# Sixteen bytes between the channel chunks of a matmul operand in a hybrid pool, convolution, attention and expert trunk

## The reference, cut to what matters

```
for l in range(DEPTH):
    h = rms_norm(x, g_mix[l])
    u = jnp.einsum('bsd,dc->bsc', h, w_in[l])
    y_pool, y_conv, y_attn, gates = ...
    merged = (gates[:, :, 0] * jnp.einsum('bsc,cd->bsd', y_pool, w_br_pool[l]) + ... )
    x = x + jnp.einsum('bsd,de->bse', merged, w_out[l])
    h = rms_norm(x, g_ffn[l])
    x = x + (swiglu(h, ...) if l % 2 == 0 else moe_ffn(h, ...))
```

## Time and profile before

| | us |
|---|---|
| median of 2 runs | 1742.53 |
| the two runs | 1741.94 and 1743.11 |
| span of the profiled execution, first to last instruction | 1738.7 |
| TensorE busy (matmuls) | 1689.6 (97%) |
| TensorE weight loads busy | 1454.0 (84%) |
| VectorE busy | 1283.2 (74%) |
| ScalarE busy | 1053.3 (61%) |

### The profile page before, as it was taken

How to read it: one execution, slowest core, us unless ns; L and a number is a source line. 1 busy time by engine, 2 the same in 40 slices (tenths; PEclk the granted TensorE clock), 3 DMA queues, 4 the chain that set the end, 5 groups by cost and what they waited for, 6 DMA issues and landing times.

```text
span 1738.7 us, 25143 instructions
## 1 busy us (share of the span) xinstructions
PE 1689.6 (97%) x9630; PEld 1454.0 (84%) x9630; DVE 1283.2 (74%) x1078; ACT 1053.3 (61%) x902; POOL 51.5 (3%) x52
## 2 busy tenths in 40 slices
PE   7999989999899998999999999999999999999998
PEld 7988889999898888788788788788788788788787
DVE  5964754444696475787887887887887887887886
ACT  5544444444554445677677677677677677677675
POOL 0131000000013000000000000000000000000000
PEclk9999999999999998999999999999999999999999
DMA  9533445555353342699899899899899899899893
GB/s 331 172 123 105 142 142 170 193 174 165 122 170 122 116 141 86 253 369 342 316 363 335 323 366 329 333 364 329 319 375 330 327 368 331 324 370 330 322 373 146
DMA packets 231292, 452.46 MB, mean 260 GB/s; under 512 B 6992, under 2 KB 80720, under 8 KB 231120
## 3 DMA queue, kind: packets, MB, share of 16 engines
q1 hardware_dynamic: 231248, 451.82, 73.5%
HBM read 450.74 MB, written 1.05 MB: 260 GB/s over the span
## 4 chain that ended last, share of the span: by engine, by line
PE 89%; DVE 8%; issue 2%; ACT 1%; DVEq 0%; DMA 0%; ACTq 0%
PE bank L269 27%; PE bank L271 27%; PE bank L270 27%; DVE w_low L259 3%; PE bank L1237 2%; PE bank L1253 1%; DVE xacc L929 1%; PE bank L997 1%; DVE h_full L690 1%; PE bank L1087 1%; DVE gate L685 1%; DVE h_full L616 0%; PE bank L1106 0%; ACT w_high L255 0%; DVE rinv L606 0%
## 5 line engine op out<-in xcount | busy, mean ns | idle before, releaser
L259 DVE TENSOR_TENSOR w_low<-raw,w_high 128x2048 fp32r<-128x2048 f32 x427 | 975.5, 2290 | 323.8 <-ACT w_high L255 322.8
L255 ACT ACTIVATE w_high<-raw 128x2048 fp32r<-128x2048 f32 x427 | 818.3, 1917 | 441.6 <-PE bank L271 439.6
L269 PE MATMUL bank<-w_high,hg_high 128*128 128x512 f32 x896 | 358.5, 400 | 7.6 <-DVE w_low L259 7.6
L270 PE MATMUL bank<-w_low,hg_high 128*128 128x512 f32 x896 | 353.9, 395 | 0.0
L271 PE MATMUL bank<-w_high,hg_low 128*128 128x512 f32 x896 | 353.9, 395 | 0.0
L269 PE MATMUL bank<-h_high,w_high 128*128 128x256 f32 x1056 | 307.3, 291 | 9.4 <-DVE h_low L611 4.8
L270 PE MATMUL bank<-h_low,w_high 128*128 128x256 f32 x1056 | 300.9, 285 | 0.0
L271 PE MATMUL bank<-h_high,w_low 128*128 128x256 f32 x1056 | 300.9, 285 | 0.0
L269 PEld LDWEIGHTS bank<-h_high,w_high 128*128 128x128 f32 x1056 | 204.8, 194 | 15.0 <-issue 9.6
L269 PEld LDWEIGHTS bank<-w_high,hg_high 128*128 128x128 f32 x896 | 169.3, 189 | 47.6 <-DVE w_low L259 9.7
L270 PEld LDWEIGHTS bank<-h_low,w_high 128*128 128x128 f32 x1056 | 205.0, 194 | 1.6 <-issue 1.4
(11 more groups left out here) (225 smaller groups left out, 1587.8 us busy)
## 6 DMA issues: line engine op xcount, KB each, us to landing
raw<-exp_w SPq DMA_DIRECT2D x336, 1024.0 KB, 5.2
raw<-w_in SPq DMA_DIRECT2D x42, 1024.0 KB, 5.1
raw<-ffn_w SPq DMA_DIRECT2D x33, 1024.0 KB, 5.2
raw<-w_out SPq DMA_DIRECT2D x8, 1024.0 KB, 5.3
raw<-w_br_attn SPq DMA_DIRECT2D x4, 1024.0 KB, 4.9
raw<-w_br_pool SPq DMA_DIRECT2D x2, 1024.0 KB, 5.2
raw<-w_br_conv SPq DMA_DIRECT2D x2, 1024.0 KB, 5.4
cst<-consts SPq DMA_DIRECT2D x1, 1280.0 KB, 13.5
```

Of the source, the lines that this page charges most:

```text
L255: nc.scalar.activation(wh[c % SPLIT][:], raw[c % RAW][:], ACT.Copy).then_inc(s["high_done"], 1)
L259: nc.vector.tensor_tensor(wl[c % SPLIT][:], raw[c % RAW][:], wh[c % SPLIT][:].bitcast(F32), ALU.subtract).then_inc(s["split_done"], 1)
L269: pe.matmul(dst, lh, rh, start=start and i == 0, stop=False)
L270: pe.matmul(dst, lh, rl, start=False, stop=False)
```

## The change

The tile gets 260 instead of 256 elements per chunk, and the kernel works on a view of the first 256. A chunk still is 1024 bytes in one run; the step from chunk to chunk becomes 1040 bytes, so chunk k lies 16k bytes further than before. The tile grows by 128 bytes, and all tiles declared behind it (`h_low` and on) move up by 128 bytes. No instruction is added, removed or moved.

```
+STAGGER = 4
...
-        hH = sb("h_high", [P, KC, S], F32R)
+        hH = sb("h_high", [P, KC, S + STAGGER], F32R)[:, :, 0:S]
         hL = sb("h_low", [P, KC, S], F32R)
```

## The result

The changed kernel takes 1713.88 us (median of 2 runs, 1713.27 to 1714.50) against 1742.53 us, a ratio of 0.9842 with a 95% interval of 0.9813 to 0.9871: 28.6 us faster. The forecast was 1735, 7.7 us faster. The direction was right and the range held, but only a quarter of the size was foreseen, and most of the gain comes from a term that stood in the sum as 0. Part of the 28.6 us is the clock of the single runs. At like clocks the change is worth some 24 to 26 us. `STAGGER = 4` adds a line, so L269 to L271 of before are L270 to L272 here.

What follows compares the result with a forecast made beforehand. TensorE, busy 97% of the span, was taken as the bound, so only matmul rates could matter. Terms of -7.0, -1.4, 0 and +0.7 summed to -7.7 us, giving 1735 us against 1742.53, range 1712 to 1766 for 8 in 10.

Steps and rivals of the forecast that it cites:

- the second rival: `hH` matmuls fall to 109 ns as load and stream miss each other: -23.2 us, 1719, or 1708 with `hL`; chance 17%.
- the likeliest case: The forecast itself, 7.7 us faster at 1735 us, given 40%, with its own range of 1722 to 1750.
- if any change comes from a stage without `h_high`: Sign that the forecast is wrong: stages not using `h_high` change; the expert groups should stay at 400, 395, 396 ns.
- The inference from four rates: Next weights' load and present stream hinder each other in SBUF, more on the same residue (120 ns), less otherwise (113 to 119).
- Terms 1 to 3: `products` matmuls: `hH` moving -7.0 us, `hL` moving -1.4 us, both as stationary operand -0.9 us, left inside the rounding.
- Term 4: Experts' 4032 matmuls of 512 columns: distance goes from 128 to 0 modulo 512, rate stays 232.5 ns; 0, bounds -10 to +30 us.
- Term 5: `g` in the dense `down` goes to the residue of `h`, +0.7 us; `y` stays at 64 modulo 128, 0.
- Term 6: ScalarE's 24 writes and VectorE's 24 reads become two runs of 256, at most 4 ns each; 0, bounds 0 and +0.2 us.
- Nothing moves: Rival: the extra over 106.7 ns is not due to place; `h` stays 120.0, experts 232.5, time 1742.5; chance 25%.
- The conflict goes wholly: Rival: with every chunk on another residue, `hH` matmuls fall to 109 ns, 1719 us, or 1708 if `hL` follows; chance 17%.
- The experts pay: Rival: the 128 byte shift puts `hg` and `g` on the weights' residue, expert matmuls take 240 ns, 1765 us; chance 10%.
- Odd starts cost: Rival: `hH` chunks beginning off a multiple of 64 bytes need more fetches, +10.6 us, 1753; chance 8%.

## Why the prediction was right or wrong

**What bounds the kernel.** Right. The busy time that TensorE lost, 27.4 us, came back as 26.3 us of span.

**The number.** The range of 1712 to 1766 held by luck, for its lower end had been set by the second rival, `hH` at 109 ns, which did not happen; the likeliest case's own range, 1722 to 1750, did not hold. By one of its own signs ("if any change comes from a stage without `h_high`") the forecast was wrong, for the experts gave most of the change. A small slip besides: the prediction added 3.8 us to the span, but in every run on record whose span is listed the time is some 2.1 us longer (1714.50 against 1712.4), so its span of 1731.0 stood for a time of 1733.

**The reading.** The inference from four rates, that the distance between the streamed and the loaded operand weighs on the price, is borne out by the experiments that moved only one side and the one that moved both. One of the four rates was luckier than it looked: the 113.3 ns of `y` is one of two at which it settles in the same place. That the two reads meet in SBUF stays an inference: the runs show the dependence on the distance, not the place where the reads meet.

**Terms 1 to 3, `hH` and `hL`.** Right in kind, twice too large. Terms 1 and 2 stood as -7.0 and -1.4 us, with 116.7 and 118.7 ns. Measured at 2.4 GHz are 118.6 and 118.5 ns: 2112 x -1.3 = -2.8 us and 1056 x -1.3 = -1.4 us, and the stationary uses of term 3 add -0.6. The 8.1 us of busy time look like a hit, but 3 us of them are the clock. The split was off as well: the stagger gives -6 alone, and nothing beside the shift of `hL`. The rates of the two halves are not independent, since they are streamed by turns. The form that was foreseen is there: in the dense `up` of the kernel after the steps of `h` go from 113 to 125 ns and repeat every 24 matmuls to within half a nanosecond on the mean, where before each was 120.

**Term 4, the experts.** This is the step that failed. It stood as 0, bounds -10 to +30, and measured -19.0 us. The mechanism was named (128 to 0 modulo 512), the number was taken from the earlier trace rows, four clearing matmuls at distance 0 that took 232.5 ns each. They still do. After the change a matmul that has just started after a break runs at 232 too, and only after about a dozen comes to the settled 226.7. A run of four never shows the settled rate. Another analogue stood in the trace: `h` at distance 0 had settled at 120.0, which is 106.7 + 13.3, and the same 13.3 on the 213.3 ns that 512 columns would take by this count is 226.7, the measured rate. But that carry is no rule, and to have made it would have been luck: at the distance 128 the extra at 256 columns is 12.1 ns (118.8) and at 512 it is 19.2 (232.5), and at 192 it is 6.7 against 20.0. The lower bound was too tight for the same reason: single steps of 230 ns, read to 10 ns, were taken as the least that could be.

**Term 5.** `g` went from 118.8 to 119.7, in the forecast direction (+0.9 ns against +1.3). `y` did not stay: 64 modulo 128 was the wrong rule. Its distance went from 192 to 64 modulo 256, and the mean from 114.9 to 117.8, +1.1 us, within the bound of 2.6; five of its six long stretches ran at 113.3 to 113.7 before, none after.

**Term 6.** Right: L369 takes 631 ns and L612 686 (medians), 1 and 2 ns more than before.

```profile
L612 DVE TENSOR_TENSOR h_low<-h_full,h_high x16: 683/686/692, 14.6 to 672.4; 128x512 fp32r<-128x512 f32 x16
...
L369 ACT ACTIVATE h_high<-h_full x16: 629/631/635, 13.9 to 671.7; 128x512 fp32r<-128x512 f32 x16
```

**The rivals.** "Nothing moves" fell with the first group. It had been drawn from the page of the Trainium skill "TensorE: Matmul & The Clock Gate", Part 2, by which loading weights takes nothing from the running matmul's reads. The runs contradict the conclusion, that no address could matter: the same `float32r` instructions run at 113 to 120 ns when only tiles are moved. Whether it is the reads that collide, no run shows. The 109.2 ns of the prediction were not that page's figure for this case: under "Back-to-back issue gap" it gives N/2.4 + 2.5 for a single matmul by itself, and says that in a stream of load and matmul pairs both set the distance. Here that stream never came to 109. "The conflict goes wholly" did not happen in the kernel after or in any of the 12 experiments; the lowest mean of a pair of tiles was 113.7. It has nearly the measured time (1719 and 1708 against 1714) for the wrong reason. "The experts pay" had the place right and the sign wrong: it took the slowest of the 256 column distances to be the slowest at 512 as well, where it is the fastest. "Odd starts cost" fell for the chunks of `hH`, which with the stagger alone ran faster (117.9) than without (119.9).

## What to carry to other kernels

In this kernel, where TensorE is the bound with `float32r` operands, the address distance between the tile that streams and the tile that is loaded beside it, modulo 256 bytes, was worth up to 5% of a matmul at 256 columns and 3% at 512. Where that is so, try pads ahead of the tiles (0 for 512 columns, 192 for 256 columns here) before changing anything in the loops, and look at the tiles behind an enlarged one as well as at the one that was edited. When a rate is carried over from another place in a trace, count how many matmuls in a row it rests on, and look whether other stretches of the same group show it too. And before a few microseconds are put down to a change, compare the granted clock of the two profiles.

## What the runs showed of the hardware that was not expected

- The best distance depends on the number of columns: of the six that were tried, 192 is the best at 256 columns (113.7 to 116.7 ns) and with 32 and 224 the worst at 512 (233.1 to 233.3).
- At 192 and 256 columns an unbroken stretch settles at one of two rates, 113.3 or 117.8 ns, in the same kernel and with the same addresses; which one it will be, the runs don't explain.
- Counted at one column per cycle of 2.4 GHz, an estimate, settled rates are 106.7 + 6.7 = 113.3, 106.7 + 13.3 = 120.0 and 213.3 + 13.3 = 226.7 ns: 16, 32 and 32 cycles over the columns. What takes these cycles, no run tested.
- The two distances that are no multiple of 64 gave means of 117.9 to 118.4 ns at 256 columns and 233.1 to 233.3 ns at 512, so 32 bytes beside the best place lose all of the gain at 512 columns.
